# One fused two-block kernel on one core: the latent units of the even mixer, row block 3 first instead of row block 0 first

## What is computed

```python
score = where(causal, sum_t(w_idx * relu(q_idx @ k_idx.T)), -inf)
sel = top_k(score, 128)                       # 128 keys for each query
la = ql @ c_kv[sel].T + rel_bias[...]         # 8 latent heads, rank 128
oa = softmax(la) @ c_kv[sel]                  # "a" units: latent attention
lb = qb @ k_b.T + cum_f - cum_f_keys          # 8 heads of width 64
ob = softmax(where(causal, lb, -inf)) @ v_b   # "b" units: gated attention
out = concat(oa @ w_uv, ob) @ w_o
```

## Time and profile before

| what | us |
|---|---|
| median of 3 runs (2299.24 to 2299.47) | 2299.24 |
| the profiled execution's own time | 2297.08 |
| its span, first to last instruction | 2295.5 |
| PE busy (92% of the span) | 2122.0 |
| DVE busy (54%) | 1245.0 |
| ACT busy (38%) | 876.3 |
| POOL busy (15%) | 334.8 |
| mean granted clock of TensorE, share of full speed | 0.958 |

### The profile page before, as it was taken

How to read it: one execution, slowest core, us unless ns; L and a number is a source line. 1 busy time by engine, 2 the same in 40 slices (tenths; PEclk the granted TensorE clock), 3 DMA queues, 4 the chain that set the end, 5 groups by cost and what they waited for, 6 DMA issues and landing times. The chain is left out here.

```text
span 2295.5 us, 27519 instructions
## 1 busy us (share of the span) xinstructions
PE 2122.0 (92%) x9734; PEld 1678.5 (73%) x9734; DVE 1245.0 (54%) x1922; ACT 876.3 (38%) x1345; POOL 334.8 (15%) x412
## 2 busy tenths in 40 slices
PE   8999879999999899899999979997877788999996
PEld 6666547888888677688888848884656667888885
DVE  3666437788667655766653352116749934333323
ACT  4433534444422443444442242227554524222222
POOL 0033312010000210100000030004039802000001
PEclk9999899999999999999999989997988889999998
DMA  5211002566445222132332212210000022333330
GB/s 190 76 44 37 1 29 67 183 197 193 151 156 157 95 83 83 56 101 92 100 116 96 81 37 92 64 46 1 1 10 10 13 79 66 101 91 101 110 101 37
DMA packets 52624, 191.78 MB, mean 84 GB/s; under 512 B 5792, under 2 KB 8512, under 8 KB 52288
## 3 DMA queue, kind: packets, MB, share of 16 engines
q1 hardware_dynamic: 44672, 163.07, 22.2%
q0 software_dynamic: 7344, 27.27, 3.8%
q10 hardware_dynamic: 528, 0.40, 0.1%
HBM read 187.05 MB, written 3.67 MB: 83 GB/s over the span
## 5 line engine op out<-in xcount | busy, mean ns | idle before, releaser
L196 PE MATMUL psum<-xH,w_hi 128*128 128x512 f32 x1800 | 719.0, 399 | 48.2 <-DVE xL L1297 23.5
L196 PE MATMUL psum<-xL,w_hi 128*128 128x512 f32 x1800 | 707.9, 393 | 0.0
L196 PE MATMUL psum<-xH,w_lo 128*128 128x512 f32 x1800 | 707.6, 393 | 0.0
L166 DVE TENSOR_TENSOR w_lo<-w_raw,w_hi 128x1024 fp32r<-128x1024 f32 (+1 forms) x273 | 353.4, 1295 | 443.9 <-ACT w_hi L160 443.9
L160 ACT ACTIVATE w_hi<-w_raw 128x1024 fp32r<-128x1024 f32 (+1 forms) x273 | 303.1, 1111 | 398.6 <-PE psum L196 394.1
L196 PEld LDWEIGHTS psum<-xH,w_hi 128*128 128x128 f32 x1800 | 342.0, 190 | 147.9 <-DVE xL L1297 38.4
L196 PEld LDWEIGHTS psum<-xH,w_lo 128*128 128x128 f32 x1800 | 342.1, 190 | 72.8
L196 PEld LDWEIGHTS psum<-xL,w_hi 128*128 128x128 f32 x1800 | 342.8, 190 | 67.9 <-issue 0.5
L196 PE MATMUL psum<-hidH,w_hi 128*128 128x512 f32 x528 | 206.2, 391 | 0.0
L196 PE MATMUL psum<-hidH,w_lo 128*128 128x512 f32 x528 | 205.4, 389 | 0.0
L196 PE MATMUL psum<-hidL,w_hi 128*128 128x512 f32 x528 | 205.4, 389 | 0.0
(11 more groups left out here) (312 smaller groups left out, 2538.0 us busy)
## 6 DMA issues: line engine op xcount, KB each, us to landing
w_raw<-in_up SPq DMA_DIRECT2D x132, 512.0 KB, 3.5
w_raw<-in_down SPq DMA_DIRECT2D x48, 704.0 KB, 4.0
mod_raw<-in_mod POOLq DMA_DIRECT2D x48, 512.0 KB, 3.8
w_raw<-in_sb_in SPq DMA_DIRECT2D x26, 512.0 KB, 3.5
w_raw<-in_ev_in SPq DMA_DIRECT2D x23, 512.0 KB, 3.6
w_raw<-in_od_in SPq DMA_DIRECT2D x20, 512.0 KB, 3.5
w_raw<-in_ev_out SPq DMA_DIRECT2D x8, 512.0 KB, 3.5
w_raw<-in_od_out SPq DMA_DIRECT2D x8, 512.0 KB, 3.4
```

What stands on the lines that cost most here:

```text
L166: nc.vector.tensor_tensor(w_lo[:, s % SPLIT, 0:w.cols], raw[:, s, 0:w.cols], w_hi[:, s % SPLIT, 0:w.cols].bitcast(F32), ALU.subtract).then ...
L196: mm = nc.tensor.matmul(acc, a[:, slot % SPLIT, cut], b[:, k0 + k, :], start=start and n == 0, stop=stop and n == 2)
```

## The change

The list of a units goes through the row blocks from 3 to 0 instead of 0 to 3. Names i and h of a unit stay the row block and the head; places that meant the position in the list (semaphore counts, the two halves of qlT, xH and xL blocks of the row outputs) are computed from the position n or from NB - 1 - n. POOL waits for all three selections before the first a unit, where it waited for none there, and for one more at each following row block. No instruction is added or removed, the shapes and counts are the same, and each b unit is where it was.

```diff
--- before.py
+++ after.py
@@ -391,7 +391,7 @@
             "prob_t", "prob_out", "pv_b", "o_b_hi", "o_b_lo", "b5", "b5_out", "o_a_lo", "zero")}
         TURN, OUT, PV = 3, 4, 5
         units = [("b", i, 2 * m + e) for m in range(HEADS // 2) for i in range(NB) for e in range(2)]
-        units += [("a", i, h) for i in range(NB) for h in range(HEADS)]
+        units += [("a", NB - 1 - n, h) for n in range(NB) for h in range(HEADS)]
 
 
         GROUP_FROM, PARTS = 13, ((0, 1, 2), (3, 4, 5), (6, 7))
@@ -495,9 +495,8 @@
                         nc.gpsimd.affine_select(out=X[:, blk(i)], in_=X[:, blk(i)], compare_op=ALU.is_ge, fill=NEG,
                                                 base=0, pattern=[[-1, P]], channel_multiplier=1).then_inc(a["addend"], 1)
                     else:
-                        if h == 0 and i:
-                            pool.wait_ge(a["mneg"], i)
-                        elif h == 0:
+                        if u == UNITS:
+                            pool.wait_ge(a["mneg"], NB - 1)
                             pool.wait_ge(s_far, 1)
                             pool.wait_ge(s_near, 16 * HEADS)
                         mneg = scores[i] if i else causal
@@ -582,9 +581,9 @@
                     act.wait_ge(a["b5"], row_output(i, g))
                     nc.scalar.activation(dst, bank[7][:, :].rearrange("p (h q) -> p h q", h=4), ACT.Copy).then_inc(a["b5_out"], 1)
 
-                def queries_out(i, half):
-                    act.wait_ge(a["index"], row_queries(i, half))
-                    nc.scalar.activation(qlT[:, i % 2, 4 * half:4 * half + 4, :], bank[6][:, :].rearrange("p (h q) -> p h q", h=4),
+                def queries_out(n, half):
+                    act.wait_ge(a["index"], row_queries(n, half))
+                    nc.scalar.activation(qlT[:, n % 2, 4 * half:4 * half + 4, :], bank[6][:, :].rearrange("p (h q) -> p h q", h=4),
                                          ACT.Copy, scale=float(HD) ** -0.5).then_inc(a["relu"], 1)
 
                 def prob_out(u):
@@ -596,8 +595,9 @@
                     else:
                         g = h // 4
                         dst = pT_a[g][:, 0:i + 1, h % 4, :]
-                        if h % 4 == 0 and i:
-                            act.wait_ge(a["b5"], row_output(i - 1, g))
+                        n = (u - UNITS) // HEADS
+                        if h % 4 == 0 and n:
+                            act.wait_ge(a["b5"], row_output(n - 1, g))
                     if u == 0:
                         act.wait_ge(s_skew, 16)
                     act.wait_ge(a["prob_t"], u + 1)
@@ -633,7 +633,7 @@
                         if i and k == 5:
                             row_out(i - 1, 1, oaT[:, 4:8, :])
                         if i and k == 7:
-                            row_out(i - 1, 2, xH[:, 0:4, blk(i - 1)])
+                            row_out(i - 1, 2, xH[:, 0:4, blk(NB - i)])
 
                 s = 0
                 for c in range(GROUP_FROM, w.n):
@@ -754,8 +754,9 @@
                     if s >= UNITS and k == 0 and i >= 2:
                         r = i - 2
                         dve.wait_ge(a["b5_out"], row_output(r, 2))
-                        nc.vector.tensor_tensor(xL[:, 0:4, blk(r)], bank[7][:, :].rearrange("p (h q) -> p h q", h=4),
-                                                xH[:, 0:4, blk(r)].bitcast(F32), ALU.subtract).then_inc(a["o_a_lo"], 1)
+                        q = blk(NB - 1 - r)
+                        nc.vector.tensor_tensor(xL[:, 0:4, q], bank[7][:, :].rearrange("p (h q) -> p h q", h=4),
+                                                xH[:, 0:4, q].bitcast(F32), ALU.subtract).then_inc(a["o_a_lo"], 1)
 
                 s = 0
                 for c in range(GROUP_FROM, w.n):
@@ -840,9 +841,10 @@
                         l, r = hT[rows(h), head_queries(h), blk(i)], hT[rows(h), head_keys(h), 0:n]
                     else:
                         pe.wait_ge(a["ttr"], u - 3)
+                        row = (u - UNITS) // HEADS
                         if h == 0:
-                            pe.wait_ge(a["relu"], row_queries(i, 1))
-                        l, r = qlT[:, i % 2, 4 * (h % 2) + h // 2, :], hT[:, EV_CKV, 0:n]
+                            pe.wait_ge(a["relu"], row_queries(row, 1))
+                        l, r = qlT[:, row % 2, 4 * (h % 2) + h // 2, :], hT[:, EV_CKV, 0:n]
                     nc.tensor.matmul(logits_bank(u)[:, 0:n], l, r, start=True, stop=True).then_inc(a["logits"], 1)
 
                 def turn(u):
@@ -873,8 +875,9 @@
                     else:
                         pe.wait_ge(a["b5_out"], row_output(i, 0))
                     pe.wait_ge(a["prob_out"], UNITS + HEADS * i + 4 * g + 4)
-                    for j in range(i + 1):
-                        mm = nc.tensor.matmul(bank[7][:, :], c_tm[:, j, :], pT_a[g][:, j, :, :], start=j == 0, stop=j == i)
+                    top = NB - 1 - i
+                    for j in range(top + 1):
+                        mm = nc.tensor.matmul(bank[7][:, :], c_tm[:, j, :], pT_a[g][:, j, :, :], start=j == 0, stop=j == top)
                     mm.then_inc(a["b5"], 1)
 
                 def queries(i, half):
@@ -887,7 +890,7 @@
                             tile_there(t)
                     for h in range(half, HEADS, 2):
                         mm = nc.tensor.matmul(bank[6][:, blk(h // 2)], w_uk[rows(h), h // 2, :],
-                                              hT[rows(h), EV_QA + h // 2, blk(i)], start=True, stop=True)
+                                              hT[rows(h), EV_QA + h // 2, blk(NB - 1 - i)], start=True, stop=True)
                     mm.then_inc(a["index"], 1)
 
                 def outputs_a(i):
```

## The result

| kernel | median, us | runs |
|---|---|---|
| before | 2298.62 (2294.67 to 2300.10) | 22 |
| changed | 2301.28 (2297.83 to 2303.90) | 22 |

The ratio is 1.0014, with a 95% interval of 1.0008 to 1.0021: the change costs 1.8 to 4.8 us, by the medians 2.7. The forecast was a gain of 1 us. The time lies in the forecast range and under the 0.2% of its middle case, but the sign is the other one, and the interval excludes no change.

What follows compares the result with a forecast made beforehand. PE's work was taken as most of the path before the last logits, the chain itself as the drain's bound. +6.45 ahead of the last logits, -9.4 drain, +1.9 low clock gave -1.05 us: 2298.2 from 2299.24, range 2293.5 to 2304.

Steps and rivals of the forecast that it cites:

- middle case: Whole kernel: no difference over 0.2% (4.6 us) from before, 2295 to 2302 us, chance 0.60.
- The start: POOL's wait for three selections before the first latent addend: cost 0, with 8.8 us for a 1.3 us addend.
- The work ahead of the last logits: PE's logits, transposes and latent products moved ahead of the last logits: +6.9 us, 0 hidden in waits.
- The waits: PE's waits ahead of the last logits: 9.9 us against 10.35, so -0.45.
- The drain: Behind the last logits (L): 9.4 us shorter at full clock, second product ending L + 6.35; half clock gives back 1.9.
- The clock behind the drain: At ev_out's start: the 3.78 us at half clock taken as unchanged.
- The slower rival: PE at 1.2 GHz through most of row 0 and the drain, first low stretch longer: +7.4, 2305.6 us; chance 0.16.
- The faster rival: Clock stays up in the drain (-1.9), half the added products fall into waits (-2.5): 2293.8 us; chance 0.24.
- The third: Rival: rows ahead pay what the drain saves to within a us, 2299 us; shares the forecast's chance of 0.60.

Runs made afterwards that it cites:

- e3: Kernel before with unused 512-column idle matmuls in PE's drain waits and 12 small ones ahead of ev_out: 2295.88 us, ratio 0.9987.
- e4: Kernel before with two wide pairs of POOL operations, results unused, between row block 3's selection and the first addend: 2297.88 us, ratio 0.9998.
- e11: Kernel before with one narrow and one wide two-input POOL operation, the wide timed to begin just ahead of DVE's line 747: 2298.78 us, one execution.
- e12: Kernel before with idle matmuls: two ahead of the first queries, others in PE's waits, the drain and at ev_out: 2289.01 us, ratio 0.9959.
- e13: Changed kernel with POOL's first addend late and idle matmuls in PE's waits, two ahead of the first queries: 2292.64 us, ratio 0.9971.
- e5: Changed kernel with row block 3's latent products cut to their first key block: 2294.71 us, ratio 0.9985.
- e14: Changed kernel repeated as it is: 2301.67 us, ratio 1.0012.
- e1: Changed kernel with POOL's first latent addend held until the first xL of a b output is written: 2298.51 us, ratio 1.0002.
- e2: Changed kernel with unused 512-column idle matmuls in PE's drain waits and 12 small ones ahead of ev_out: 2299.73 us, ratio 1.0005.
- e8: Kernel before with idle matmuls: three ahead of the first queries, one ahead of step 32, others in the drain and at ev_out: 2290.76 us, ratio 0.9971.

## Why the prediction was wrong

**The start** was the first step that failed: "Cost 0", argued from POOL having 8.8 us to spare. It had, and it was never late. But a wide addend ran where a narrow one had begun behind DVE's row, and it held DVE at line 747: 0.96 us for 0.41, PE's wait 2.41 for 1.86. Another 0.5 stands in step 31, where the clock fell sooner in its course (first queries to step 32: 6.84 against 6.34); in the old order without collision that part takes from 6.08 (e3) to 7.48 (e4), so it isn't shown that the collision brings it on. I asked who waits for POOL, and not what POOL's work does to the engine beside it. The Trainium skill, SBUF — State Buffer, section on two separate sides, says that DVE and GpSimd share one pair of ports under an exclusive lock, which a DVE operation contends for in a two-port mode or with two inputs in SBUF, and that whichever starts first blocks the other for its whole instruction. e4 and e11 agree in both directions, 0.94 for 0.72 on POOL and 0.89 for 0.41 on DVE; in the changed kernel DVE was held although its row begins 0.03 us ahead of POOL's.

**The work ahead of the last logits** was right. +6.9 was forecast; PE's busy time rose from 58.38 to 65.12 us, +6.74, in which a shorter low stretch at the beginning and a new one in row 0 about cancel. In e12 and e13, less their idle matmuls of 0.92 us each (two and five), it is 54.2 and 60.9, +6.7. That no more than a small part of the products hides was right as well (e5, within its uncertainty).

**The waits** were the second step that failed: -0.45 forecast, +0.82 measured, and +1.6 in e12 and e13 (10.5 and 12.1). Rows 3 and 2 were right or better (1.10 and 2.82 for 1.8 and 2.74). Rows 1 and 0 have 3.23 and 4.02 for 2.29 and 3.1: each narrow row begins with the turns and copies of the wider row before it and with the wait for xL (0.76 at 303.64), so it waits for wide work and does narrow work meanwhile. PE's timeline of the changed kernel has the turn of a row 2 unit in row 1's steps:

```profile
284.18 0.52 PE L856 MATMUL psum<-ident,logits 128*128 128x128 f32 x3 [1.10 <-DVE logits L747]
```

Four waits of this kind, 3.4 us in all, are for DVE's normalisation (line 747), where every wait of a turn had been for ACT's copies before. I had taken a row's waits as its own and not as those of its predecessor's tail.

**The drain** was sized right and credited wrongly. To the end of the second product L + 6.35 was forecast for full clock, and it was at L + 7.85 with the clock down before it, where I allowed 7.3 (in e14 it is L + 7.09, so that the size of this miss is chance); the outputs took 1.97 as forecast. But I took 9.4 us off a drain of 15.74 that had a low stretch in it, against one without; e4's drain of the old order, at full clock, is 20.00 where this one was 21.70. At full clock in both orders the difference is 7.7 (21.75 less 14.09).

**The clock behind the drain** was taken "as it was", 3.78 us. It was 5.28, which is 0.75 us; the clock had been down through most of the drain already. That this is the reason isn't shown: the low clock reaches 4.7 and 5.0 us into ev_out in e1 and e14, but in the old order 3.0 in e11 and 6.1 in e4, whose drain had the full clock. The slower rival had named this, row 0 and the drain, and priced it at 7.4 together with a longer first stretch. Its mechanism came true in part, 3 us in row 0 instead of all of it, and the first stretch went the other way in this trace (in e14 it was 17 us). By the Trainium skill (TensorE: Matmul & The Clock Gate, Part 4) transposes don't count as busy in the way that matmuls do, and I had concluded that by this alone the clock would be low through row 0. From 308.2 to 318.2 it was 1.00, with PE busy 6.31 of 10 us, so the conclusion was wrong. The rule itself isn't tested there, since transposes were only 2.11 us of that work.

Together: 0.55 + 0.5 at the start, 1.3 of waits, 0.55 in the drain and 0.75 behind it are 3.6 us on top of the forecast -1.05, about the 2.7 to 3.2 measured. The trace's own 3.7 of span has some 0.3 ahead of the edited steps and 1 behind the stage that I count as chance. This is one trace added up, and not a division that the runs show: its 0.5 in step 31, 0.55 in the drain and 0.75 behind it vary with the execution by more than themselves, while e1 gained 2.8 us by its median from the collision's end alone, more than the 0.55 that its trace shows. How the 3 us divide between collision, clock and order stays open, but for the order's own 0.7 at full clock.

The faster rival (clock up, half of the products hidden) fell with e5 and e2. The third, that the two effects balance, was nearly right about the order itself, and that is a different thing from the kernel.

## What to carry to other kernels

Reversing wide and narrow work moves a cost: at full clock the drain got 7.7 us shorter and the part ahead of it 8.3 longer, since the last product of a pipeline doesn't vanish when another is put last. When an edit makes an engine work longer or earlier than it did, look at who runs beside it at that time, and not only at who waits for it. And where an engine's clock falls after short waits, price both drains at the same clock, then look at what the next stage starts with; filling those waits was worth some three times what the change of order cost, even with idle matmuls that were too long in places.

## What the runs showed of the hardware that was not expected

- A two-input POOL operation and a DVE tensor_scalar from SBUF held each other, and with starts a few hundredths of a microsecond apart either could be the one held: 0.96 and 0.89 us for 0.41 on DVE, or 0.94 for 0.72 on POOL.
- One wait of 1.86 us (2.4 with the collision) ahead of narrow work was followed by 10 to 17 us at 1.2 GHz although PE was then busy nearly without a gap; with two or three 512 column matmuls in the wait the clock stayed at 2.4 GHz in all six traces that had them (e8 had one stretch of 3.4 us later on). Two of them cost nothing: the first queries begin at 230.95 in e12 and 231.05 before, and it is 4.7 us from there to step 32, where it was 6.34.
- Stages of the same code behind the edit, begun at full clock, took 1964.1 to 1968.5 us in ten traces. A single trace can't settle a question of 3 us for the whole program, and a stretch of it can.
